# Turned activations moved by 64 bytes in a partition, the first feed-forward matrix in 256-column steps, one-hots two units later

## What is computed

```python
def first_block(x, ...):
    h = _rms_norm(x, g_pre_mix); proj = h @ w_in              # attention inputs, latents, gates
    merged = gates_a * (o_a @ w_branch_a) + gates_b * (o_b @ w_branch_b)
    x = x + _rms_norm(merged @ w_out, g_post_mix)
    h2 = _rms_norm(x, g_pre_mlp)
    m = jnp.square(jax.nn.relu(h2 @ w_up)) @ w_down            # 1024 -> 4096 -> 1024
    return x + _rms_norm(m, g_post_mlp)

def second_block(x, ...):
    proj = rms_norm(x, norm1_g) @ w_in                        # gated mixing and dilated attention
    x = x + mix @ w_out
    x = x + peer(rms_norm(x, norm2_g), w_query, sub_keys, expert_u, expert_v)

def peer(xb, w_query, sub_keys, expert_u, expert_v):          # 16384 experts, 8 heads, 16 of them each
    s1, i1 = top_k(scores of the first keys, 16); s2, i2 = top_k(scores of the second keys, 16)
    sc, ci = top_k(s1[..., None] + s2[..., None, :], 16); e = i1[ci // 16] * 128 + i2[ci % 16]
    act = gelu(einsum('td,thkd->thk', xb, expert_u[e]))
    return einsum('thk,thkd->td', softmax(sc) * act, expert_v[e])
```

## Time and profile before

| | us |
|---|---|
| median of 3 runs (1290.05 to 1290.81) | 1290.5 |
| the profiled execution, its own time | 1290.7 |
| its span from first to last instruction | 1288.9 |
| PE busy | 1279.4 |
| DVE busy | 952.9 |
| ACT busy | 689.5 |

### The profile page before, as it was taken

How to read it: one execution, slowest core, us unless ns; L and a number is a source line. 1 busy time by engine, 2 the same in 40 slices (tenths; PEclk the granted TensorE clock), 3 DMA queues, 4 the chain that set the end, 5 groups by cost and what they waited for, 6 DMA issues and landing times.

```text
span 1288.9 us, 21561 instructions
## 1 busy us (share of the span) xinstructions
PE 1279.4 (99%) x8375; PEld 1156.8 (90%) x8375; DVE 952.9 (74%) x1733; ACT 689.5 (53%) x1161; POOL 34.7 (3%) x29
## 2 busy tenths in 40 slices
PE   9999999999999999999999999999999999999998
PEld 8899988888878889999999999999988888888886
DVE  6776568884467767999999777777776676766676
ACT  6666467553455754444454555555555444555545
POOL 0000030000020010000000000000000000000000
PEclk9999999999999999999999999999999999999999
DMA  8543456656656445577767656566677767776763
GB/s 267 164 135 128 132 179 198 195 181 198 193 165 222 131 144 174 148 243 232 235 218 229 217 184 208 185 193 198 196 271 272 243 243 245 244 241 240 242 242 114
DMA packets 72805, 260.53 MB, mean 202 GB/s; under 512 B 8256, under 2 KB 9024, under 8 KB 72448
## 3 DMA queue, kind: packets, MB, share of 16 engines
q1 hardware_dynamic: 71232, 255.25, 61.1%
q0 software_dynamic: 1040, 3.34, 0.8%
q10 hardware_dynamic: 432, 0.56, 0.1%
HBM read 240.25 MB, written 18.87 MB: 201 GB/s over the span
## 4 chain that ended last, share of the span: by engine, by line
PE 95%; DVE 2%; ACT 1%; POOL 1%; issue 0%; DVEq 0%; ACTq 0%
PE ps L1096 27%; PE ps L483 16%; PE ps L491 12%; PE ps L492 12%; PE ps L493 12%; PE ps L502 4%; PE ps L1057 2%; PE ps L505 2%; PE ps L549 1%; PE ps L536 1%; PE ps L680 1%; POOL wlo L2419 1%; PE ps L542 1%; PE ps L530 1%; PE ps L1016 1%; PE ps L513 0%
## 5 line engine op out<-in xcount | busy, mean ns | idle before, releaser
L1644 DVE TENSOR_TENSOR wlo<-raw,whi 128x1024 fp32r<-128x1024 f32 (+2 forms) x410 | 497.6, 1215 | 262.8 <-ACT whi L1133 258.5
L1133 ACT ACTIVATE whi<-raw 128x1024 fp32r<-128x1024 f32 (+2 forms) x421 | 441.9, 1050 | 396.5 <-PE ps L1096 168.9
L491 PE MATMUL ps<-T,whi 128*128 128x256 f32 x1264 | 363.9, 288 | 0.0
L492 PE MATMUL ps<-T,whi 128*128 128x256 f32 x1264 | 357.2, 283 | 0.0
L493 PE MATMUL ps<-T,wlo 128*128 128x256 f32 x1264 | 357.2, 283 | 0.0
L1096 PE MATMUL ps<-whi,T 128*128 128x512 f32 x1024 | 315.5, 389 | 0.0
L492 PEld LDWEIGHTS ps<-T,whi 128*128 128x128 f32 x1264 | 242.1, 192 | 0.0
L491 PEld LDWEIGHTS ps<-T,whi 128*128 128x128 f32 x1264 | 242.0, 191 | 0.0
L493 PEld LDWEIGHTS ps<-T,wlo 128*128 128x128 f32 x1264 | 241.9, 191 | 0.0
L1096 PEld LDWEIGHTS ps<-whi,T 128*128 128x128 f32 x1024 | 192.2, 188 | 39.9 <-DVE wlo L1644 0.2
L1096 PE MATMUL ps<-wlo,T 128*128 128x512 f32 x512 | 199.2, 389 | 0.0
(11 more groups left out here) (326 smaller groups left out, 1403.6 us busy)
## 6 DMA issues: line engine op xcount, KB each, us to landing
raw<-in_expert_u_dram SPq DMA_DIRECT2D x128, 512.0 KB, 3.7
raw<-in_expert_v_dram SPq DMA_DIRECT2D x128, 512.0 KB, 3.8
raw<-in_w_up_dram SPq DMA_DIRECT2D x32, 512.0 KB, 4.2
raw<-in_w_down_dram SPq DMA_DIRECT2D x32, 512.0 KB, 4.2
acts<-stage SPq DMA_DIRECT2D x32, 512.0 KB, 4.2
stage<-acts SPq DMA_DIRECT2D x30, 512.0 KB, 3.3
raw<-in_w_in_dram SPq DMA_DIRECT2D x20, 512.0 KB, 4.2
raw<-in_w_gate_dram SPq DMA_DIRECT2D x16, 512.0 KB, 3.5
```

What stands on the lines that cost most here:

```text
L491: e.matmul(dst, whi[:, h, sl], xh[:, k, :], start=k == 0, stop=False)
L492: e.matmul(dst, whi[:, h, sl], xl[:, k, :], start=False, stop=False)
L1133: e.activation(whi[:, u % NH, 0:n], raw[:, u % NR, 0:n], ACT.Copy).then_inc(*hi(u))
L1644: e.tensor_tensor(wlo[:, u % NH, 0:n], raw[:, u % NR, 0:n], whi[:, u % NH, 0:n].bitcast(F32), ALU.subtract).then_inc(*lo(u))
```

## The change

`T` becomes two tiles, `turned_h` and `turned_l`, each of 2048 elements and 32 more. There are two views of each: `TH`, `TL` begin 16 elements (64 bytes) behind the tile's start, `RH`, `RL` at its start. With the addresses of the built program, `TH` and `TL` begin at 65728 and 74048, a multiple of 128 plus 64, and `RH`, `RL` at 65664 and 73984, multiples of 128. In both a chunk is 1 KB and the chunks follow each other. Everything that `cols` streams is in `TH`, `TL`; so are the stationary chunks of the first block, of `pair` and of the last half of the second block's `w_out`. The second block's `w_in` and `expert_v` take theirs from `RH`, `RL`. Two unused tiles of 64 bytes (`gap2`, `gap3`) bring `MH`, `ML` and `AH`, `AL` to multiples of 128 (`MH` to 85632, `ML` to 118400). `OA`, `OB`, `CQ`, `CK` stay at a multiple plus 64.

`wide_cols` goes: `w_up`'s 30 units use `cols`, 24 matmuls of 256 columns, and wait for `wlo` at their start. ACT takes PSUM through Relu, squares it into `MH`; DVE squares and subtracts. `UB1` is 1.35 and is spent in the first 67 units; `EXP_AT`, `TURN_AT`, `HOT_FROM` are 45, 67, 68.

```diff
-UB1 = 1.42
+UB1 = 1.35
-EXP_AT, TURN_AT, HOT_FROM = 42, 65, 66
+EXP_AT, TURN_AT, HOT_FROM = 45, 67, 68
-        T = sb(ctx, "T", [128, 8, 2, 256], F32R)
-        TH, TL = T[:, :, 0, :], T[:, :, 1, :]
+        turned_h = sb(ctx, "turned_h", [128, 2048 + 32], F32R)
+        turned_l = sb(ctx, "turned_l", [128, 2048 + 32], F32R)
+        TH, TL = (x[:, 16:2064].rearrange("p (k n) -> p k n", n=256) for x in (turned_h, turned_l))
+        RH, RL = (x[:, 0:2048].rearrange("p (k n) -> p k n", n=256) for x in (turned_h, turned_l))
...
+        sb(p2, "gap2", [128, 16])
...
+        sb(p3, "gap3", [128, 16])
...
-            def wide_cols(u, x, b, ks):
-                h = u % NH
-                e.wait_ge(*hi.at(u))
-                for k in ks:
-                    e.matmul(ps[b][:, :], whi[:, h, k * 128:k * 128 + 128], x[:, k, :, :], start=k == 0, stop=False)
-                whole(u)
-                for k in ks:
-                    m = e.matmul(ps[b][:, 0:256], wlo[:, h, k * 128:k * 128 + 128], x[:, k, 0, :], start=False, stop=k == 7)
-                return m
...
             for n in range(2, 32):
+                whole(UP + n)
...
-                    e.wait_ge(*relu_d.at(f"sq{n - 4}" if n < 6 else f"sum{n - 4}"))
-                wide_cols(UP + n, T, (n + 2) % 4, range(8)).then_inc(*used(UP + n))
+                    e.wait_ge(*relu_a.at(f"r{n - 4}"))
+                cols(UP + n, 0, 8, TH, TL, ps[(n + 2) % 4][:, 0:256], range(8)).then_inc(*used(UP + n))
...
-                        m = rows(u, 2, 512, TH, TL, [[ps[b][:, :]], [ps[b + 1][:, :]]], k - j, 8, both(j))
+                        m = rows(u, 2, 512, RH, RL, [[ps[b][:, :]], [ps[b + 1][:, :]]], k - j, 8, both(j))
...
-                for k, (x, w) in enumerate(((TH, whi), (TH, wlo), (TL, whi))):
+                for k, (x, w) in enumerate(((RH, whi), (RH, wlo), (RL, whi))):
...
-            def relu_take(n):
+            def relu(n):
+                b = n % 4
                 e.wait_ge(*(turned.at(f"h2.p{n}") if n < 2 else used.at(UP + n)))
                 if n >= 4:
-                    e.wait_ge(*relu_d.at(f"sq{n - 4}"))
-                at = 0 if n < 2 else 256
-                copy(mr[:, n % 4, :], ps[(n + 2) % 4][:, at:at + 256]).then_inc(*relu_a(f"r{n}"))
-            def relu_high(n):
-                e.wait_ge(*relu_d.at(f"sq{n}"))
-                copy(MH[:, n, :], mf[:, n % 4, :]).then_inc(*relu_a(f"high{n}"))
+                    e.wait_ge(*relu_d.at(f"low{n - 4}"))
+                e.activation(mr[:, b, :], ps[(n + 2) % 4][:, 0:256], ACT.Relu).then_inc(*relu_a(f"r{n}"))
+                e.wait_ge(*relu_a.at(f"r{n}"))
+                e.activation(MH[:, n, :], mr[:, b, :], ACT.Square).then_inc(*relu_a(f"high{n}"))
...
-                if n >= 2:
-                    e.tensor_tensor(mr[:, b, :], ps[(n + 2) % 4][:, 0:256], mr[:, b, :], ALU.add).then_inc(*relu_d(f"sum{n}"))
-                    e.wait_ge(*relu_d.at(f"sum{n}"))
-                e.scalar_tensor_tensor(out=mf[:, b, :], in0=mr[:, b, :], scalar=0.0, in1=mr[:, b, :], op0=ALU.max,
-                                       op1=ALU.mult).then_inc(*relu_d(f"sq{n}"))
+                e.tensor_tensor(mf[:, b, :], mr[:, b, :], mr[:, b, :], ALU.mult).then_inc(*relu_d(f"sq{n}"))
...
-                if n < 64:
+                if n < TURN_AT:
                     pull(UB1)
```

More of the change, by code:

```diff
@@ L443, in build @@
         relu_d = signal("relu_d", (
[5 rows of a table removed]
-            "sum31 sq31 low30 low31").split())
[3 rows of a table added]
+            "low27 sq28 low28 sq29 low29 sq30 low30 sq31 low31").split())
         fold_d = signal("fold_d", ["00", "10", "01", "11"])
@@ L929, in high_rows @@
                     e.wait_ge(*low.at(f"h3.{k0 + j}{t}"))
-                    e.matmul(ps[t][:, :], TH[:, k0 + j, sl], whi[:, h, j * 512:j * 512 + 512], start=k0 + j == 0, stop=False)
-                    e.matmul(ps[t][:, :], TL[:, k0 + j, sl], whi[:, h, j * 512:j * 512 + 512], start=False, stop=False)
+                    e.matmul(ps[t][:, :], RH[:, k0 + j, sl], whi[:, h, j * 512:j * 512 + 512], start=k0 + j == 0, stop=False)
+                    e.matmul(ps[t][:, :], RL[:, k0 + j, sl], whi[:, h, j * 512:j * 512 + 512], start=False, stop=False)
             def low_rows(u, k0, t):
@@ L937, in low_rows @@
                 for j in range(2):
-                    m = e.matmul(ps[t][:, :], TH[:, k0 + j, sl], wlo[:, h, j * 512:j * 512 + 512], start=False, stop=False)
+                    m = e.matmul(ps[t][:, :], RH[:, k0 + j, sl], wlo[:, h, j * 512:j * 512 + 512], start=False, stop=False)
                 return m
@@ L1325, in high_tile @@
                         e.wait_ge(*low.at(f"{name}{c - 2}1"))
-                    copy(TH[:, c, t * 128:t * 128 + 128], ps[b][:, at:at + 128], gain(c)).then_inc(
+                    copy((RH if name == "h3." else TH)[:, c, t * 128:t * 128 + 128], ps[b][:, at:at + 128], gain(c)).then_inc(
                         *high(f"{name}{c}{t}"))
@@ L1414, in scalar_program @@
             split(UP + 4)
-            relu_take(0)
-            relu_take(1)
-            relu_high(0)
+            relu(0)
+            relu(1)
             for n in range(3, 32):
-                relu_take(n - 1)
                 split(UP + n + 2)
-                relu_high(n - 2)
+                relu(n - 1)
                 if n == 8:
@@ L1425, in scalar_program @@
                     row_root("out", r2_st)
-            relu_take(31)
-            relu_high(30)
-            relu_high(31)
+            relu(31)
             e.wait_ge(*norm_d.at("rsq"))
@@ L1923, in low_tile @@
             def low_tile(name, t, chunks, gain):
+                dh, dl = (RH, RL) if name == "h3." else (TH, TL)
                 for c in chunks:
@@ L1926, in low_tile @@
                     e.wait_ge(*high.at(f"{name}{c}{t}"))
-                    e.scalar_tensor_tensor(out=TL[:, c, sl], in0=ps[b][:, at:at + 128], scalar=gain(c),
-                                           in1=TH[:, c, sl].bitcast(F32), op0=ALU.mult, op1=ALU.subtract).then_inc(
+                    e.scalar_tensor_tensor(out=dl[:, c, sl], in0=ps[b][:, at:at + 128], scalar=gain(c),
+                                           in1=dh[:, c, sl].bitcast(F32), op0=ALU.mult, op1=ALU.subtract).then_inc(
                         *low(f"{name}{c}{t}"))
@@ L2028, in vector_program @@
             relu(1)
-            relu_low(0)
             for n in range(3, 32):
+                split(UP + n + 2)
                 relu(n - 1)
-                split(UP + n + 2)
-                relu_low(n - 2)
                 if n == 9:
```

14 lines of the change are left out of this document (6 added, 8 removed), and 14 rows, old and new, of tables (relu_a, relu_d).

## The result

The changed kernel takes 1292.7 us against 1290.5: a ratio of 1.0017 with a 95% interval of 1.0010 to 1.0024. It was forecast at 1263.3. The profiled executions stand at spans of 1290.4 and 1288.9 us, +1.5.

A forecast was written before the change was run, and what follows sets the result against it. PE, busy 99% of the span, bounds the kernel: number of matmuls times distance between starts. -25.3 - 2.2 - 0.8 + 0.6 + 0.3 = -27.4 us gives 1263.3; own range 1261 to 1267, stated range 1260 to 1273.

The forecast's parts named there:

- The step that failed: 256-column matmuls streaming `T`: moved 64 bytes further, they would start every 113.3 ns like those over `OB`, instead of 120.0.
- The term of -25.3 us: 3792 matmuls in gate, `w_query` and `expert_u` units, 6.7 ns less each, all on PE; bounds -8.7 and nothing.
- `w_up`: 30 units in 256-column matmuls: 2.72 us a unit for 2.79, -2.2 us; +2.6 us if steps stay at 120.0 ns.
- `expert_v`, counted at nothing: It keeps both places; its high and low parts lie further apart, which was counted at nothing.
- the sign of it: The prediction is wrong if `expert_v` leaves 226 to 227 ns because `RH` and `RL` lie 8 KB apart.
- the term for the 288 matmuls: 512-column matmuls in `w_in`, `w_out` and half the second `w_out`, stationary chunks now `TH`, `TL`: +0.6 us, bounds 0 and +1.2.
- `w_down` -0.8: `MH`, `ML` at a multiple of 128: 384 matmuls at 2.0 ns less, -0.8 us, bounds 0 and -1.2.
- DVE's lead at the start of `expert_u`: DVE's split stays ahead of the faster PE in the first units, by only 0.4 us, so nothing is added.
- The remainder of unit 4: In `expert_u`, DVE's remainder for unit 4 lands about 0.4 us ahead of PE.
- The wait for the third one-hot group: PE arrives earlier and waits about 0.5 us for DVE's third one-hot group, up from 0.16: +0.3 us.
- Rival 1: Only part of the step goes (117.7 ns): -8.7 us for the 3792 matmuls, about 1283 us; chance 0.09.
- Rival 2: The place isn't the cause: the 3792 matmuls keep 120.0 ns, `w_up` pays +2.6 us, 1293.9 us; chance 0.09.

The follow-up runs named there:

- the sweeps: Kernel before, operands of the expert stages moved in 64-byte steps, one alone, then both; one alone: `expert_u` 113.5 to 119.9 ns, `expert_v` 226.8 to 233.3 ns.
- units of 2.72 us: Changed kernel with streamed chunks 64 bytes back, loaded ones at the weights' place, also for `w_out`: 1266.97 us, ratio 0.9817.
- the fine sweep: Kernel before, moving `T` in `expert_u` and stationary `T` in `expert_v` shifted in 16-byte steps; at 128 bytes `expert_v` had 233.4 ns.
- both pairs of traces above: Kernel before with 192 bytes ahead of `T` (1281.9 and 1275.5 us); fastest kernel with 256 bytes ahead of `OA` (1266.7 and 1273.4 us).

## Why the prediction was wrong

**The step that failed** is "the form, the stationary operand and the place modulo 128 are those of `OB`". It read one difference between two rows and took 128 bytes for the period. What the sweeps show is a dependence on the distance to the stationary operand, of period 256. `OB` lay at 64; modulo 128 `TH` and `TL` both got its place, modulo 256 only `TL` did, and `TH`, which two thirds of the matmuls stream, came to lie on the other side of the weights. With both halves at distance 64 a step of `expert_u` takes 117.8 ns, with both at 192 it takes 113.3 or 117.8. The changed kernel, with one half at each, got 117.8 for the mean of its three products, and its 20 executions form one group (1292.0 to 1294.0). From start to next start `TH` on `whi` had 118.3 ns, `TL` on `whi` 116.7, `TH` on `wlo` 118.3: `TL` at the place of `OB` did not get its 113.3. No run tells whether the matmuls between hold it up or whether all of them are at the upper level.

The step had a second fault. It took 113.3 ns as the price of a place, and one place can have two. The trace of the kernel before held the case: the 18 matmuls of `w_uq` ahead of those in the earlier trace rows, with the same tiles at the same distance, start every 113.5 ns (17 steps in 1.93 us), and those of the earlier trace rows every 117.7.

```profile
60.94 0.28 PE L483 MATMUL ps<-whi,CQh 128*128 128x256 f32 x1
...
62.87 0.28 PE L483 MATMUL ps<-whi,CQl 128*128 128x256 f32 x1
```

The term of -25.3 us came out as about -7: 3792 times 2.2 ns is -8.3, and 1.2 of that is missing in `expert_u`, which shows -5.55 for 3072 x 2.2 = -6.8. A unit of its second half went from 3.38 to 3.35 us, since its steps were at 119.4 ns already before and not at 120.0.

**`w_up`** was sized by the same step. With 120 ns the edit costs +2.6 us (measured +2.6); in the changed kernel its steps are 116.9 ns on average and a unit is 2.81 us for 2.79; with 113.3 it is 2.72, as forecast.

**`expert_v`, counted at nothing**, cost 6.8 us, the largest single error beside the step. The prediction gave no reason for the nothing. `RL` was still at a multiple of 128, which by the rule of 128 was the same place; modulo 256 it lies 128 off the weights. The prediction named the sign of it as what would make it wrong and gave it no price. The rows of `w_down` (228.9 ns, its operands at distance 64) and of the second `w_in` (226.9, distance 0) already held two values of the curve.

**Too small by half** was the term for the 288 matmuls whose stationary chunks are `TH`, `TL`: +0.6 for about +1.2, the far end of its bounds. `w_in` rose from 227.8 to 231.9 ns a step in its three long stretches (102 matmuls) and `w_out` from 227.6 to 231.9 (84), twice the 2.0 ns that were taken. The sweep has 233.3 ns for the distance of `TH` and 229.0 for that of `TL`, 231.9 on average. The second `w_in`, counted with `expert_v` at nothing, has +0.3 in its longest stretch.

**The right ones.** `w_down` -0.8 (measured -0.80). DVE's lead at the start of `expert_u` held: no wait of PE's names the split there, neither in the changed kernel nor with units of 2.72 us. The remainder of unit 4, forecast 0.4 us ahead of PE, landed 1.1 us ahead in the changed kernel and 0.8 with units of 2.72. The wait for the third one-hot group was put at 0.5 us and is 0.26 in the changed kernel, whose units are longer than forecast, and 0.41 with units of 2.72. Not foreseen: `OA` and `OB`, at an unchanged distance, went from 113.3 to 117.8 ns, +0.9 us.

**The rivals.** Rival 1 had the step (117.7) and by it -7.6 us. With `expert_v` +6.8, `OA` and `OB` +0.9 and the 1.5 us by which `expert_u` gained less than 3072 x 2.3 ns, that is +1.6; the spans differ by +1.5. That it fits so closely is in part luck: its term for the stationary chunks is 0.6 us too small and the one for `w_up` 0.5 too large. Rival 2 had the time nearly to the microsecond (1293.9 for 1292.7) by luck, not by its cause: the steps did change, and a gain and a loss of about 7 us cancelled. By the Trainium skill's page "SBUF — State Buffer", section "SBUF: two separate sides", by which within the engine side only the port shared by VectorE and GpSimd causes contention, no shift would have moved anything. The pads of 64 and 192 bytes, with nothing else changed, moved the time by +5.2 and -14.9 us, so the measurement decides against that rule here.

## What to carry to other kernels

Where PE is the path and the steps are short, sweep the start of one operand in steps of 64 bytes inside one kernel, before reading a rule out of two rows: one run gave the curve in steps of 64, and two points leave many periods open. Work out the place of the high and of the low part, each by itself. Price a shift for every use of the tile, as moving and as stationary operand: the best distance for 256 columns (192 bytes) was not the best for 512 (0), and two views of one tile, 64 bytes apart, gave both. And look at all executions of a kernel: two levels of the same step show as two groups of times.

## What the runs showed of the hardware

A matmul's step depends on where its moving operand lies to its stationary one modulo 256 bytes. With 512 columns it was 226.8 ns at distance 0, 229.0 at 64 (233.0 in one stage), 232.4 at 128 (233.4 in the fine sweep), 233.3 at 192; with 256 columns 119.9 at 0, 118.7 at 128, and either 117.8 or 113.3 at 64 and 192. The granted clock was 1.00 in all of these windows, so it is not the clock. The load for the next matmul begins with the present one, as in `expert_v` after the change:

```profile
1000.29 0.40 PE L1088 MATMUL ps<-wlo,turned_h 128*128 128x512 f32 x1
1000.29 0.19 PEld L1088 LDWEIGHTS ps<-whi,turned_l 128*128 128x128 f32 x1
1000.52 0.40 PE L1088 MATMUL ps<-whi,turned_l 128*128 128x512 f32 x1
1000.52 0.19 PEld L1088 LDWEIGHTS ps<-whi,turned_h 128*128 128x128 f32 x1
```

There only the low half lay off, and two products of three were longer (389, 396, 397 ns); from start to next start they have 226.7 (`RH` on `whi`), 232.5 (`RH` on `wlo`, with the load of `RL` beside it) and 234.2 (`RL` on `whi`). That suggests that the load which runs beside a matmul counts as well as its own; no run separates the two. That both read the same memory at once would fit, and was only argued.

What stays open is what puts a stretch on one of the two levels. It is not the place modulo 512 alone (the gap of 256 bytes before `OA`), and no place settles it alone, since executions of one program differ. In `expert_u` a stretch kept its level until something interrupted it, over 1560 matmuls: in both pairs of traces above the two agree in the first unit (117.8 and 117.8, 113.3 and 113.3) and part behind it, where 16 matmuls for the scores stand between.
